# A two-block kernel on one core: the cross-attention memory loaded in feature quarters, with its transposes and splits moved between key chunks and modulation sums

## The chip, the cores and the metric

The kernel runs on one core of one Trainium2 chip. The metric is the device time of one execution in microseconds (us). The profile is one execution, recorded by the hardware profiler; its times count from the start of its span.

## The reference

Two transformer blocks run one after the other on 256 tokens with 2048 features, all in float32. What matters here is the start of the work. The program's first products belong to the cross attention of the second block (its keys depend only on the memory `mem_2`, so they can be made first) and to the modulation of the first block:

```python
# second block: cross attention over 256 memory rows
rms_norm_2(mem, norm_mem)            # (256, 2048)
k, v = split_cols_2(mem_n @ w_kv_cross, (512, 512))
# first block: modulation of context and latent
m = jax.nn.silu(cond) @ w[:, :n * D_MODEL] + b[:n * D_MODEL]
uc = ctx_s * (1.0 + sc_c) + sh_c     # then uc @ w_in_e ...
```

## The kernel before

Every large product is made to float32 precision out of three passes. A weight chunk is 512 input features by 512 output columns, 1 MB. SyncE's queue (SP) loads it into one of four slots of `weights_raw`; ScalarE (ACT, `hi`, L861) rounds it to `weights_hi`; VectorE (DVE, `lo`, L1706) subtracts to get `weights_lo`; TensorE (PE, `chunk`, L2928) then does 24 matmuls on it: 4 feature tiles by 2 token halves by 3 passes. The activations are split the same way, into `acts_hi` (L949) and `acts_lo` (L1778), after PE has transposed them (`transposes`, L3001). Four side banks take the transposes; one job is two feature tiles by two token halves, so 4 transposes.

The start of the program, which the change touches, works on three things:

- **The memory**, `memory_first` (MEM0), 256 rows by 2048 features, 2 MB. It needs 8 transpose jobs. Jobs 0 and 1 are the features of key chunk 0, jobs 2 and 3 those of key chunk 1, and so on.
- **The key chunks** 0 to 3 of `w_kv_cross` (stage `mem_k`), 1 MB each.
- **The modulation chunks** m0, m1, ... of `w_ada` (256 input features by two blocks of 512 columns each, 1 MB, loaded as two DMAs of 512 KB). They go into four slots of `modulation_weights`; PE sums them with `cond_sums` (L3024, 8 matmuls in the trace for one chunk: 4 instructions of two float32 passes), and only when chunk m is summed (`cond_used`) may SP load m+4 into its slot. m7 completes the first quarter of the modulation, m15 the second. After m7 ACT and DVE copy the rows, PE turns them into columns (`cond_cols`, L3013), and the context and latent pieces (`context_piece`, `latent_piece`, 512 KB each, loaded by GpSimd's queue, POOL) are modulated with them.

SP issues in the order written by hand in `block.sync`: it waits inside the list, so a load behind a waiting load waits too. `MEM_LOADS` and `KV_LOADS` say behind which modulation chunk a key chunk or a chunk of `w_in_e` is issued. In POOL's list the first context piece waits for `cond_used` 2 and the first latent piece for `cond_used` 6. PE's order is set by `stream(st["mem_k"], after={...})`: after key chunk 0 come jobs 4 to 7 and m0, m1; after chunk 1 come m2, m3; after chunk 2 come m4 to m7 and the columns; then chunk 3. Then the context and latent products (L3078) alternate with m8, m9 and so on, two at a time, down to m15.

A second copy of the memory, `memory_natural` (MEMN), is loaded much later, inside stage `mix`, ahead of chunk 6 of `w_mix_out` on the same queue.

Of the kernel before, what the change touches and what calls it, by code (L numbers as in the profile page):

```python
# [15 lines left out]
P = 128  # L16
T = 256
D = 2048
NB = 512
# [123 lines left out]
def build(nc, a, out, stop=None):  # L143
# [256 lines left out]
    st = {}  # L400
# [41 lines left out]
    J, n = {}, 0  # L442
# [83 lines left out]
        return CONDR[:, m % 4]  # L526

    COND_BANK = (2, 7, 5, 7)
    MEM_LOADS = {1: 2, 3: 3}
    KV_LOADS = {7: 0, 8: 1} | {8 * q + k: 4 * q + n - 4 for q in range(1, 4) for n, k in enumerate((1, 3, 5, 7), 1) if (q, n) != (1, 1)}  # L530
    KV_FIRST = 1 + max(KV_LOADS.values())
    GATE_AT = list(range(6, 19)) + [20, 23, 26]
    landed = [S(f"chunk_landed{i}") for i in range(4)]
    cond_landed = [S(f"cond_landed{i}") for i in range(8)]
    COND_IN = 16 * 2 * KT // 4
    FIRST_RANK_IN = COND_IN + 16 * (2 * KT // 8 + 1)
    PLAIN_BANK = (0, 2)
# [62 lines left out]
    @block.sync  # L600
    def _(eng):
        def load(s, blk, kc, g, slot=None):
            if not isinstance(g, int) or g >= 4:
                eng.wait_ge(lo_ready, g - 3)
            sl = slot if slot is not None else g % 4 if isinstance(g, int) else kc
            src = s.view((kc + s.rot) % s.kc, blk)
            if s.name == "lora":
                eng.dma_start(RAW[:, sl, :, 0:288], src[0]).then_inc(cond_landed[sl], 16)
                eng.dma_start(RAW[:, sl, :, 288:368], src[1]).then_inc(landed[sl], 16)
                return  # L610
            eng.dma_start(RAW[:, sl, :, 0:s.n], src).then_inc(landed[sl], 16)

        def memory(dst):
            for h in range(2):
                eng.dma_start(dst[:, :, h, :], a["mem"][0][h * P:(h + 1) * P, :].rearrange("p (b n) -> p b n", n=NB))\
                   .then_inc(S("mem_in"), 16)

        def by_chunk():

            eng.wait_ge(S("a_ab_ready"), 1)  # L620
            sa = a["scratch_a"].rearrange("(u c) t s -> c t u s", c=4)
            for c in range(4):
                r = slice(C * c, C * (c + 1))
                eng.dma_start(sa[c], AAB[r, :, r]).then_inc(S("a_ab_stored"), 16)
            eng.wait_ge(S("a_ab_stored"), 64)
            bank_full(eng, J["aqT"] + 3)
            eng.dma_start(AC[:, :, :], a["scratch_a"]).then_inc(S("a_by_chunk_in"), 16)
            eng.wait_ge(S("inverse_ready"), 1)
            eng.dma_start(a["scratch_t"], TC[:, :, :]).then_inc(S("inverse_stored"), 16)
            eng.wait_ge(S("inverse_ready"), 2)  # L630
            eng.dma_start(a["scratch_a"], TCR[:, :, :]).then_inc(S("rows_stored"), 16)
            eng.wait_ge(S("inverse_stored"), 16)
            eng.wait_ge(S("inverse_zeroed"), 2)
            sb = a["scratch_t"].rearrange("(u c) s t -> c s u t", c=4)
            for c in range(4):
                eng.dma_start(TT[C * c:C * (c + 1), :, C * (c % 2):C * (c % 2) + C], sb[c]).then_inc(S("inverse_in"), 16)
            eng.wait_ge(S("rows_stored"), 16)
            sr = a["scratch_a"].rearrange("(u c) t s -> c t u s", c=4)
            for c in (0, 2):
                eng.dma_start(TA[C * c:C * (c + 1), :, :], sr[c]).then_inc(S("rows_in"), 16)  # L640

        for s in stages:
            if s.name == "delta_y":
                by_chunk()
            if s.view is None:
                continue
            if s.own_ring:
                memory(MEM0)
                for c in range(2):
                    load(st["mem_k"], 0, c, c)  # L650
                for m in range(s.kc * s.nblk):
                    if m >= 4:
                        eng.wait_ge(S("cond_used"), m - 3)
                    for e in range(2):
                        eng.dma_start(cond_chunk(m)[:, 2 * e:2 * e + 2, :], s.view(2 * (m % 8) + e, m // 8))\
                           .then_inc(cond_landed[m % 8], 16)
                    if m in MEM_LOADS:
                        load(st["mem_k"], 0, MEM_LOADS[m], MEM_LOADS[m])
                    if m in KV_LOADS:
                        c = KV_LOADS[m]  # L660
                        load(st["ctx_kv"], KV_BLOCKS[c % 4], c // 4, st["ctx_kv"].g0 + c)
            elif s.name == "mem_k":
                pass
            elif s.name == "ctx_kv":
                for c in range(KV_FIRST, s.nblk * s.kc):
                    load(s, KV_BLOCKS[c % 4], c // 4, s.g0 + c)
            elif s.plain:
                for m in range(s.kc * s.nblk):
                    if m < 4:
                        eng.wait_ge(lo_ready, s.g0 - 3 + m)  # L670
                    elif m < 8:
                        eng.wait_ge(chunk_used, s.g0 + 2)
                    else:
                        eng.wait_ge(S("plain_used"), m - 7)
                    eng.dma_start(RAW8[:, m % 8], s.view(m % s.kc, m // s.kc)).then_inc(cond_landed[m % 8], 16)
                eng.wait_ge(S("plain_used"), s.kc * s.nblk - 4)
            elif s.loop and not s.rot:
                with eng.Fori(0, s.nblk) as i:
                    for kc in range(4):
                        load(s, i, kc, s.g0 + 4 * i + kc)  # L680
            else:
                for c, (blk, kc) in enumerate(s.order):
                    if s.name == "mix" and c == 0:
                        bank_full(eng, J["R1"] + 1)
                    if s.name == "mix" and c == 2:
                        eng.wait_ge(S("delta_y_full"), 1)
                    if s.name == "mix" and c == 6:
                        eng.wait_ge(S("y_delta"), 2)
                        memory(MEMN)
                    load(s, blk, kc, s.g0 + c, c % 4)  # L690
        if not stop:
            for h in range(2):
                rows = out[0, h * P:(h + 1) * P, :].rearrange("p (b n) -> p b n", n=NB)
                for name, b in (("out_first", 0), ("out_last", 2)):
                    eng.wait_ge(S(name), h + 1)
                    eng.dma_start(rows[:, b:b + 2, :], OUTN[:, b:b + 2, h, :]).then_inc(S("stored"), 16)
            eng.wait_ge(S("stored"), 64)
# [152 lines left out]
    def _(eng):  # L850
# [225 lines left out]
        hi(s, s.g0, 0, 0)  # L1076
        first_memory_hi(2, 3)
        hi(s, s.g0, 0, 1)
        first_memory_hi(4, 5, 6, 7)
        hi(s, s.g0, 0, 2)  # L1080
        rms_squares(MEM0, 2, MSQ)
        hi(s, s.g0, 0, 3)
        cond_rows(0)
# [616 lines left out]
    def _(eng):  # L1700
# [192 lines left out]
        lo(s, s.g0, 0, 0)  # L1893
        first_memory_lo(2, 3)
        lo(s, s.g0, 0, 1)
        first_memory_lo(4, 5, 6, 7)
        lo(s, s.g0, 0, 2)
        inverse_rms(2)
        lo(s, s.g0, 0, 3)
        cond_rows(0)  # L1900
# [1001 lines left out]
    def _(eng):  # L2902
# [114 lines left out]
        def cond_sums(*chunks):  # L3017
            for m in chunks:
                q, kp = m // 8, m % 8
                if kp == 0 and q >= 2:  # L3020
                    eng.wait_ge(S("acts_moved"), 2 * (q - 2) + 1)
                eng.wait_ge(cond_landed[m % 8], 32 * (q + 1))
                for j in range(4):
                    ins = eng.matmul(BANKS[32 * j:32 * j + 2, COND_BANK[q], :], CF[:, 2 * kp + j // 2, :],  # L3024
                                     cond_chunk(m)[:, j, :], start=(kp == 0), stop=(kp == 7))
                ins.then_inc(S("cond_used"), 1)
# [1 line left out]
        def natural(buf):  # L3028
            return lambda f, h: buf[:, f // 4, h, (f % 4) * P:(f % 4 + 1) * P]

        def first_memory(*jobs):
            transposes("memK", natural(MEM0), jobs=jobs)

        eng.wait_ge(S("consts_in"), 16)
        eng.wait_ge(S("mem_in"), 32)
        first_memory(0, 1, 2, 3)

        def first_columns():
            cond_sums(4, 5, 6, 7)
            eng.wait_ge(S("ada0_bias_in"), 32)  # L3040
            cond_cols(0)

        stream(st["mem_k"], after={0: lambda: (first_memory(4, 5, 6, 7), cond_sums(0, 1)), 1: lambda: cond_sums(2, 3),
                                   2: first_columns})

        def first_keys():
# [127 lines left out]
        def plain_rows(m):  # L3174
# [2 lines left out]
            b, kt = m // KT, m % KT  # L3177
            if kt == 0:
                eng.wait_ge(block_out, 2 * (s.b0 + b) + 2)
            eng.wait_ge(cond_landed[m % 8], COND_IN + 16 * (m // 8 + 1))  # L3180
            for j in range(4):
                ins = eng.matmul(BANKS[32 * j:32 * j + 2, PLAIN_BANK[b], :], CF[:, kt, :], RAW8[:, m % 8, j, :],
                                 start=(kt == 0), stop=(kt == KT - 1))
# [515 lines left out]

        def memory_tiles(*jobs):  # L3700
            def step():
                eng.wait_ge(S("mem_in"), 64)
                transposes("memT", natural(MEMN), jobs=jobs)
            return step

# [114 lines left out]
```

## Time and profile before

| | us |
|---|---|
| median of 3 runs (2428.3 to 2431.14) | 2428.43 |
| the profiled execution, its own time | 2428.9 |
| its span | 2427.1 |
| PE busy in the span | 2356.6 (97%) |
| DVE busy | 1442.8 (59%) |
| ACT busy | 1088.8 (45%) |
| HBM traffic over the span | 204 GB/s |

The time of an execution is 1.8 us more than its span. PE's busy time is the sum of its matmuls; with 97% it leaves some 70 us of idle time, spread over the program.

### The profile page before, as it was taken

Reading aid. Unit: us, or ns where it says so; the run is one execution under the profiler, and the core shown is the slowest. Engines: PE = TensorE matmul, PEld = TensorE weight load, DVE = VectorE, ACT = ScalarE, POOL = GpSimd, SP = SyncE. Lnnn points to the kernel's source line nnn. Section 1 sums busy time; section 2 is a strip of 40 time slices with the busy share of each in tenths; the row PEclk is TensorE's granted clock in tenths of the full one; section 3 lists DMA queues with packets and bytes.
Section 4 is the critical chain, followed back from the end, with each engine's and each line's share of the span. In section 5 each row is a group of like instructions: output and inputs, shape, how many; then the busy total and the mean of one; then the engine's idle time right before and its main releaser. Section 6 shows DMA issues by size and latency. Waiting matters only on the chain.

```text
span 2427.1 us, 29838 instructions
## 1 busy us (share of the span) xinstructions
PE 2356.6 (97%) x12212; PEld 1913.2 (79%) x12212; DVE 1442.8 (59%) x1416; ACT 1088.8 (45%) x1147; POOL 70.5 (3%) x116
## 2 busy tenths in 40 slices
PE   7999999999999999999999998999999999999998
PEld 5667887887687788887878777788788888888886
DVE  3455567656946887566667785565555545445454
ACT  4323554534643544536555352355544334334333
POOL 1000001000000000000000000000000000000000
PEclk9999999999999999999999999999999999999999
DMA  9994678857965696555545302654566565566563
GB/s 366 333 326 144 190 236 278 267 167 268 384 205 185 232 371 207 208 192 151 185 155 173 107 10 76 229 170 158 171 180 189 186 194 187 191 191 190 191 208 121
DMA packets 234019, 496.03 MB, mean 204 GB/s; under 512 B 21568, under 2 KB 23680, under 8 KB 226848
## 3 DMA queue, kind: packets, MB, share of 16 engines
q1 hardware_dynamic: 221904, 440.04, 55.2%
q0 software_dynamic: 11984, 54.13, 6.0%
q8 instruction: 97, 1.59, 0.3%
q14 instruction: 34, 0.28, 0.0%
HBM read 487.84 MB, written 6.29 MB: 204 GB/s over the span
## 4 chain that ended last, share of the span: by engine, by line
PE 87%; DVE 7%; ACT 3%; DMA 2%; issue 1%; SPq 0%; DVEq 0%; ACTq 0%
PE banks L2928 71%; PE banks L3078 5%; PE banks L3001 2%; ACT weights_hi L861 1%; PE banks L3024 1%; DVE weights_lo L1706 1%; DMA modulation_weights<-in_w_ada 1%; DMA weights_raw<-in_w_mix_out 1%; PE banks L3253 1%; PE banks L3122 1%; PE banks L3450 1%; DVE decayed_a L2021 0%; PE banks L3058 0%; PE banks L3355 0%; DVE inverse_products L2632 0%
## 5 line engine op out<-in xcount | busy, mean ns | idle before, releaser
L1706 DVE TENSOR_TENSOR weights_lo<-weights_raw,weights_hi 128x2048 fp32r<-128x2048 f32 x348 | 795.0, 2285 | 743.4 <-ACT weights_hi L861 741.7
L861 ACT ACTIVATE weights_hi<-weights_raw 128x2048 fp32r<-128x2048 f32 x348 | 664.9, 1911 | 974.1 <-PE banks L2928 892.8
L2928 PE MATMUL banks<-weights_hi,acts_hi 128*128 128x512 f32 (+1 forms) x2032 | 801.7, 395 | 12.2 <-DVE weights_lo L1706 10.7
L2928 PE MATMUL banks<-weights_hi,acts_lo 128*128 128x512 f32 (+1 forms) x2032 | 792.2, 390 | 0.0
L2928 PE MATMUL banks<-weights_lo,acts_hi 128*128 128x512 f32 (+1 forms) x2032 | 792.1, 390 | 0.0
L2928 PEld LDWEIGHTS banks<-weights_hi,acts_hi 128*128 128x128 f32 x2032 | 383.1, 189 | 102.2 <-issue 23.8
L2928 PEld LDWEIGHTS banks<-weights_hi,acts_lo 128*128 128x128 f32 x2032 | 383.2, 189 | 79.7
L2928 PEld LDWEIGHTS banks<-weights_lo,acts_hi 128*128 128x128 f32 x2032 | 383.4, 189 | 76.6 <-issue 0.5
L2928 PE MATMUL banks<-weights_hi,hidden_hi 128*128 128x512 f32 x288 | 112.3, 390 | 0.0
L2928 PE MATMUL banks<-weights_hi,hidden_lo 128*128 128x512 f32 x288 | 112.1, 389 | 0.0
L2928 PE MATMUL banks<-weights_lo,hidden_hi 128*128 128x512 f32 x288 | 112.1, 389 | 0.0
L2928 PE MATMUL banks<-weights_hi,hidden_hi_odd 128*128 128x512 f32 x248 | 96.6, 389 | 0.0
L2928 PE MATMUL banks<-weights_hi,hidden_lo_odd 128*128 128x512 f32 x248 | 96.5, 389 | 0.0
L2928 PE MATMUL banks<-weights_lo,hidden_hi_odd 128*128 128x512 f32 x248 | 96.5, 389 | 0.0
L2928 PEld LDWEIGHTS banks<-weights_hi,hidden_lo 128*128 128x128 f32 x288 | 54.1, 188 | 11.2
L2928 PEld LDWEIGHTS banks<-weights_hi,hidden_hi 128*128 128x128 f32 x288 | 54.1, 188 | 11.2
L2928 PEld LDWEIGHTS banks<-weights_lo,hidden_hi 128*128 128x128 f32 x288 | 54.1, 188 | 11.1
L2928 PEld LDWEIGHTS banks<-weights_hi,hidden_lo_odd 128*128 128x128 f32 x248 | 46.5, 188 | 9.7
L2928 PEld LDWEIGHTS banks<-weights_lo,hidden_hi_odd 128*128 128x128 f32 x248 | 46.6, 188 | 9.6
L2928 PEld LDWEIGHTS banks<-weights_hi,hidden_hi_odd 128*128 128x128 f32 x248 | 46.5, 188 | 9.6
L3078 PE MATMUL banks<-weights_hi,context_hi 128*128 128x512 f32 x128 | 50.9, 397 | 0.0
L3078 PE MATMUL banks<-weights_lo,context_hi 128*128 128x512 f32 x128 | 49.9, 390 | 0.0
(613 smaller groups left out, 2365.5 us busy)
## 6 DMA issues: line engine op xcount, KB each, us to landing
weights_raw<-in_w_in_e SPq DMA_DIRECT2D x72, 1024.0 KB, 5.7
weights_raw<-in_w_up SPq DMA_DIRECT2D x64, 1024.0 KB, 5.5
weights_raw<-in_w_down SPq DMA_DIRECT2D x64, 1024.0 KB, 5.1
weights_raw<-in_w_in SPq DMA_DIRECT2D x44, 1024.0 KB, 5.1
modulation_weights<-in_w_ada SPq DMA_DIRECT2D x64, 512.0 KB, 10.2
raw_eight<-in_w_ada SPq DMA_DIRECT2D x32, 1024.0 KB, 7.4
weights_raw<-in_w_in_o SPq DMA_DIRECT2D x32, 1024.0 KB, 6.0
gate_piece<-in_w_ada POOLq DMA_DIRECT2D x32, 512.0 KB, 5.8
```

Of the source, the lines that this page charges most:

```text
L861: eng.activation(WHI[:, c % 2, :, 0:n], RAW[:, sl, :, 0:n], ACT.Copy).then_inc(hi_ready, 1)
L1706: eng.tensor_tensor(WLO[:, c % 2, :, 0:n], RAW[:, c % 4, :, 0:n], WHI[:, c % 2, :, 0:n].bitcast(F32), ALU.subtract).then_inc(lo_ready, 1)
L2928: ins = eng.matmul(BANKS[:, par * 2 + h, 0:s.n], x[:, t, h * P:(h + 1) * P], w[:, c % 2, k, 0:s.n], start=(kc == 0 and k == 0 and m == 0), ...
L3001: ins = eng.transpose(bank(jj)[:, (f % 2) * T + h * P:(f % 2) * T + (h + 1) * P], src(f, h), ident)
L3024: ins = eng.matmul(BANKS[32 * j:32 * j + 2, COND_BANK[q], :], CF[:, 2 * kp + j // 2, :], cond_chunk(m)[:, j, :], start=(kp == 0), stop=(kp ...
L3078: ins = eng.matmul(BANKS[:, pair * 2 + h, :], x, w[:, c % 2, k, :], start=(k == 0 and m == 0), stop=(k == 3 and m == 2))
L3122: ins = eng.matmul(bank(jj)[:, k2 * DK:(k2 + 1) * DK], KD_C[:, c0 // NB, h, c0 % NB:c0 % NB + P], NAT[:, 2 + v0 // NB, h, v0 % NB:v0 % NB ...
L3253: ins = eng.matmul(dst, DECAYED[16 + d][:, 2 * hd + k2, B * P:(B + 1) * P], S0[:, d, hd, k2, :], start=False, stop=(d == 1 and k2 == 1))
L3450: ins = eng.matmul(bank(jj)[:, q * P:(q + 1) * P], A[r, f, half * P:(half + 1) * P], B[r, f, half * P:(half + 1) * P], start=True, stop=True)
```

## The change

The memory comes as four loads of 512 KB, each a quarter of the features for both token halves, with key chunks 0 and 1 and modulation chunks between them. Each quarter has a semaphore of its own, borrowed from the modulation chunks (`cond_landed` 4 to 6). On PE the transposes run a quarter at a time, and the sums of m1 and m3 move: m1 from behind key chunk 0 to behind chunk 1, m3 from behind chunk 1 to behind chunk 2. On ACT and DVE the split of key chunk 2 goes ahead of that of memory jobs 6 and 7. The later load into `memory_natural` becomes four DMAs too.

```diff
-    MEM_LOADS = {1: 2, 3: 3}
+    MEM_LOADS = {0: 2, 3: 3}
...
+    memory_landed = [S("mem_in")] + cond_landed[4:7]
+    MEMORY_IN = [0] * 4 + [16] * 3 + [0]
...
-        def memory(dst):
-            for h in range(2):
-                eng.dma_start(dst[:, :, h, :], a["mem"][0][h * P:(h + 1) * P, :].rearrange("p (b n) -> p b n", n=NB))\
-                   .then_inc(S("mem_in"), 16)
+        def memory(dst, blocks):
+            rows = a["mem"][0].rearrange("(h p) n -> p h n", p=P)
+            for b in blocks:
+                eng.dma_start(dst[:, b, :, :], rows[:, :, b * NB:(b + 1) * NB])\
+                   .then_inc(S("mem_in") if dst is MEMN else memory_landed[b], 16)
...
-                memory(MEM0)
                 for c in range(2):
+                    memory(MEM0, (c,))
                     load(st["mem_k"], 0, c, c)
...
+                    if m < 2:
+                        memory(MEM0, (m + 2,))
                     if m in MEM_LOADS:
...
-                        memory(MEMN)
+                        memory(MEMN, range(4))
...
-        first_memory_hi(4, 5, 6, 7)
+        first_memory_hi(4, 5)
         hi(s, s.g0, 0, 2)
+        first_memory_hi(6, 7)
...
-        first_memory_lo(4, 5, 6, 7)
+        first_memory_lo(4, 5)
         lo(s, s.g0, 0, 2)
+        first_memory_lo(6, 7)
...
-        eng.wait_ge(S("mem_in"), 32)
-        first_memory(0, 1, 2, 3)
+        first_memory(0)
+        first_memory(1)
...
-            cond_sums(4, 5, 6, 7)
+            cond_sums(3, 4, 5, 6, 7)
...
-        stream(st["mem_k"], after={0: lambda: (first_memory(4, 5, 6, 7), cond_sums(0, 1)), 1: lambda: cond_sums(2, 3),
+        stream(st["mem_k"], after={0: lambda: (first_memory(2), cond_sums(0)), 1: lambda: (first_memory(3), cond_sums(1, 2)),
                                    2: first_columns})
```

**SP's queue at the program's start.** Before, the rows are:

```order
L615 DMA memory_first<-in_mem 128x4x512 x2
L611 DMA weights_raw<-in_w_kv_cross 128x4x512 x2
L655 DMA modulation_weights<-in_w_ada 128x2x512 x4
L655 DMA modulation_weights<-in_w_ada 128x2x512 x4
L611 DMA weights_raw<-in_w_kv_cross 128x4x512
L655 DMA modulation_weights<-in_w_ada 128x2x512 [waits cond_used]
```

and of the change:

```order
L618 DMA memory_first<-in_mem 128x2x512
L613 DMA weights_raw<-in_w_kv_cross 128x4x512
L618 DMA memory_first<-in_mem 128x2x512
L613 DMA weights_raw<-in_w_kv_cross 128x4x512
L658 DMA modulation_weights<-in_w_ada 128x2x512 x2
L618 DMA memory_first<-in_mem 128x2x512
L613 DMA weights_raw<-in_w_kv_cross 128x4x512
L658 DMA modulation_weights<-in_w_ada 128x2x512 x2
L618 DMA memory_first<-in_mem 128x2x512
L658 DMA modulation_weights<-in_w_ada 128x2x512 x4
L613 DMA weights_raw<-in_w_kv_cross 128x4x512
L658 DMA modulation_weights<-in_w_ada 128x2x512 [waits cond_used]
```

The whole order is now quarter 0, key 0, quarter 1, key 1, m0, quarter 2, key 2, m1, quarter 3, m2, m3, key 3; it was memory, memory, key 0, key 1, m0, m1, key 2, m2, m3, key 3. Both come to 10 MB ahead of m4, and from m4 on the queue's order is the same.

**PE from its first transpose to the modulation columns.** The 24 matmuls of each key chunk stand where "..." is. Before:

```order
L3001 MATMUL banks<-constants,memory_first 128x128 [waits mem_in,consts_in,cond_ready]
L3001 MATMUL banks<-constants,memory_first 128x128 x15
...
L3001 MATMUL banks<-constants,memory_first 128x128 [waits side_free3]
...
L3024 MATMUL banks<-modulation_weights,cond 2x512 [waits cond_landed0]
...
L3024 MATMUL banks<-modulation_weights,cond 2x512 [waits cond_landed1]
...
L3024 MATMUL banks<-modulation_weights,cond 2x512 [waits cond_landed2]
...
L3024 MATMUL banks<-modulation_weights,cond 2x512 [waits cond_landed3]
...
L3024 MATMUL banks<-modulation_weights,cond 2x512 [waits cond_landed4]
```

and of the change:

```order
L3008 MATMUL banks<-constants,memory_first 128x128 [waits mem_in,consts_in,cond_ready]
L3008 MATMUL banks<-constants,memory_first 128x128 x7
L3008 MATMUL banks<-constants,memory_first 128x128 [waits cond_landed4]
...
L3008 MATMUL banks<-constants,memory_first 128x128 [waits side_free0,cond_landed5]
...
L3031 MATMUL banks<-modulation_weights,cond 2x512 [waits cond_landed0]
...
L3008 MATMUL banks<-constants,memory_first 128x128 [waits side_free2,cond_landed6]
...
L3031 MATMUL banks<-modulation_weights,cond 2x512 [waits cond_landed1]
...
L3031 MATMUL banks<-modulation_weights,cond 2x512 [waits cond_landed2]
...
L3031 MATMUL banks<-modulation_weights,cond 2x512 [waits cond_landed3]
```

Between key chunks 0 and 1 now stand 8 transposes and one modulation chunk instead of 16 and two; between chunks 1 and 2 stand 8 transposes and m1, m2 instead of m2, m3; m3 stands behind chunk 2. From m4 on PE's order is the same.

## Rows read from the trace of the kernel before

**Rows 1.** The page: the span, and each engine's busy time.
```profile
span 2427.1 us, 29838 instructions
PE 2356.6 (97%) x12212; PEld 1913.2 (79%) x12212; DVE 1442.8 (59%) x1416; ACT 1088.8 (45%) x1147; POOL 70.5 (3%) x116
```
**Rows 2.** Waits of PE, 0 to 300 us: total, times, longest.
```profile
PE banks L3001 <- DMA memory_first<-in_mem: 10.3, 1, 10.3
PE banks L2928 <- DVE weights_lo L1706: 3.4, 1, 3.4
PE banks L3013 <- DVE modulation_rows L1828: 1.6, 1, 1.6
PE banks L3024 <- DMA modulation_weights<-in_w_ada: 1.3, 1, 1.3
```
**Rows 3.** The chain of waits, 0 to 90 us: start, us, what.
```profile
17.42 8.02 PE banks L2928 x24
25.44 1.75 PE banks L3001 x16
27.19 1.83 PE banks L3024 x16
29.02 5.67 PE banks L2928 x24
...
37.16 7.77 DMA modulation_weights<-in_w_ada
...
47.62 1.92 PE banks L3013 x16
49.54 7.20 PE banks L2928 x24
...
73.40 14.36 DMA modulation_weights<-in_w_ada
```
**Rows 4.** Windows (start:end, length; last: PE clock, DMA share, GB/s).
```profile
20.00:30.00 10.00, 10.00 (x56) 6.95 (x56) 4.25 (x9) 4.08 (x9) 0.56 (x1) 1.00 1.05 387
...
38.00:40.00 2.00, 2.00 (x11) 1.65 (x10) 1.42 (x1) 0.55 (x1) 0.00 (x0) 1.00 0.96 356
...
50.00:52.00 2.00, 2.00 (x7) 1.52 (x6) 1.85 (x5) 0.67 (x1) 0.00 (x0) 0.50 1.03 340
...
64.00:66.00 2.00, 2.00 (x17) 0.98 (x6) 1.23 (x1) 2.00 (x5) 0.00 (x0) 1.00 0.91 301
66.00:68.00 2.00, 2.00 (x11) 1.62 (x10) 0.00 (x0) 1.99 (x3) 1.41 (x3) 1.00 0.95 297
68.00:70.00 2.00, 2.00 (x11) 1.65 (x10) 1.47 (x1) 0.50 (x1) 1.71 (x2) 1.00 0.98 343
...
86.00:88.00 2.00, 0.75 (x12) 0.11 (x8) 0.00 (x0) 0.71 (x2) 0.00 (x0) 1.00 1.05 385
...
106.00:108.00 2.00, 2.00 (x14) 0.92 (x16) 2.00 (x4) 0.00 (x0) 0.00 (x0) 1.00 0.07 26
```
**Rows 5.** Timeline, the load of the constants and the first latent piece.
```profile
1.95 0.55 POOL L706 DMA_DIRECT2D constants<-in_common_consts  x1
...
44.34 0.53 POOL L717 DMA_DIRECT2D latent_piece<-in_xT  x1 [14.43 <-PE banks L3024]
```
**Rows 6.** Tile constants, 0 to 30 us: from issue to landing.
```profile
DMA to landing us min/median/max: 5.6/5.6/5.6
```
**Rows 7.** Tile modulation_weights, 0 to 110 us: from issue to landing.
```profile
DMA to landing us min/median/max: 4.0/11.3/14.4
```
**Rows 8.** Timeline of PE: matmuls of chunk 3 at its start and later.
```profile
52.38 0.63 PE L2928 MATMUL banks<-weights_lo,acts_hi 128*128 128x512 f32 x1
...
55.67 0.39 PE L2928 MATMUL banks<-weights_hi,acts_lo 128*128 128x512 f32 x1
```
**Rows 9.** The chain of waits, 1530 to 1562 us, around memory_natural.
```profile
1540.32 0.59 SPq L615
...
1541.63 10.85 DMA weights_raw<-in_w_mix_out
```

More of the change, by code:

```diff
@@ L3021, in cond_sums @@
                     eng.wait_ge(S("acts_moved"), 2 * (q - 2) + 1)
-                eng.wait_ge(cond_landed[m % 8], 32 * (q + 1))
+                eng.wait_ge(cond_landed[m % 8], MEMORY_IN[m % 8] + 32 * (q + 1))
                 for j in range(4):
@@ L3029, in natural, with first_memory @@
             return lambda f, h: buf[:, f // 4, h, (f % 4) * P:(f % 4 + 1) * P]
-        def first_memory(*jobs):
-            transposes("memK", natural(MEM0), jobs=jobs)
+        def first_memory(b):
+            eng.wait_ge(memory_landed[b], 16)
+            transposes("memK", natural(MEM0), jobs=(2 * b, 2 * b + 1))
         eng.wait_ge(S("consts_in"), 16)
-        eng.wait_ge(S("mem_in"), 32)
-        first_memory(0, 1, 2, 3)
+        first_memory(0)
+        first_memory(1)
         def first_columns():
-            cond_sums(4, 5, 6, 7)
+            cond_sums(3, 4, 5, 6, 7)
             eng.wait_ge(S("ada0_bias_in"), 32)
             cond_cols(0)
-        stream(st["mem_k"], after={0: lambda: (first_memory(4, 5, 6, 7), cond_sums(0, 1)), 1: lambda: cond_sums(2, 3),
+        stream(st["mem_k"], after={0: lambda: (first_memory(2), cond_sums(0)), 1: lambda: (first_memory(3), cond_sums(1, 2)),
                                    2: first_columns})
@@ L3179, in plain_rows @@
                 eng.wait_ge(block_out, 2 * (s.b0 + b) + 2)
-            eng.wait_ge(cond_landed[m % 8], COND_IN + 16 * (m // 8 + 1))
+            eng.wait_ge(cond_landed[m % 8], MEMORY_IN[m % 8] + COND_IN + 16 * (m // 8 + 1))
             for j in range(4):
@@ L3701, in step @@
             def step():
-                eng.wait_ge(S("mem_in"), 64)
+                eng.wait_ge(S("mem_in"), 80)
                 transposes("memT", natural(MEMN), jobs=jobs)
```

## The prediction

> **What bounds the kernel now.** I read the page first: PE is busy for 2356.6 of 2427.1 us [rows 1], so the kernel is a chain of matmuls, and a change that adds and removes none of them can only move PE's idle time. PE's waits in the first 300 us say where that lies at the start: 10.3 us for the memory, 3.4 us for the split of key chunk 0, 1.6 us for the modulation rows and 1.3 us for a modulation chunk [rows 2]. The first two, 13.7 us, are what the change reaches for.
>
> The chain of waits says who pays in the end. In the first 90 us it runs twice through a DMA of the modulation: one of 7.77 us, which ends at 44.93 (the second half of m7), and one of 14.36 us, which ends at 87.76 (m15) [rows 3]. The windows say what stands behind these: the DMA engines have a share of 1.05 at 387 GB/s from 20 to 30 us, the same share at 86 to 88 us, and fall to 0.07 only at 106 us; in between I found small gaps, at 38 and at 64 to 70 us [rows 4]. So up to m15 **the DMA engines are full**. The bytes ahead of m7 and of m15 are the same in both kernels: 10 MB ahead of m4, and the same order after it. A lead that PE gains at the start is spent in waiting for m7 and m15, unless it fills gaps.
>
> **The start.** Quarter 0 is 512 KB in place of 2 MB and is first in the queue. Then the constants, which hold the identity for the transposes, come last: issued at 1.95, 5.6 us to landing, so 7.55 [rows 5, 6]. PE begins at 7.55 in place of 10.3 [rows 2]. From the first transpose to the first matmul of key chunk 0 it takes 7.1 us now (10.3 to 17.42 [rows 3]): 4 transposes, the splits of jobs 0 and 1, the splits of the key chunk. None of that changes, so chunk 0 starts at 14.65: a lead of 2.8 us. Bounds: none if the constants are later than now, 2.8 us if not.
>
> **PE from there to m3.** Chunk 0 takes 8.02; 8 transposes 0.9 (half of 1.75); one modulation chunk 0.9 (half of 1.83); chunk 1 5.67; 8 transposes 0.9; two chunks 1.8; key chunk 2 5.67; m3 0.9 [rows 3]. That ends at 14.65 + 24.8 = 39.4. Before, m3 was summed ahead of key chunk 2: the same list with 1.75 and 1.83, 5.67, and 1.83 for m2 and m3, from 17.42, ends at 36.5. So the use of m3, which frees the slot of m7, comes **2.9 us later**, although PE started 2.8 us sooner: chunk 2 and its neighbours now stand ahead of it. The splits do not hold this up. Key chunk 2 is split ahead of memory jobs 6 and 7, and ACT is idle for several us before it.
>
> **m7.** Two conditions bound its landing. By bytes: it landed at 44.93 behind full engines, and 1 MB takes 1.05 MB / 387 GB/s = 2.7 us [rows 4], so m6 can be in by 42.2 and m7 not before 44.9. By its issue: 39.4, and then at least what the fastest 512 KB load took, 4.0 us [rows 7], of which 1.35 us is its own bytes, so 2.65 us of fixed time, then 2.7 us for both halves: 44.75. These meet within 0.2 us, so the loss of slack in the issue alone costs about nothing. But the first latent piece now comes in between. It waits for the sum of m5, behind the wait for m7 before: issued at 44.34 [rows 5]. Now m4 and m5 are summed at 39.4 + 1.8 = 41.2, its 512 KB start about 43.2, and share the engines with m7's tail. Bounds: nothing, or all of its 1.35 us. I take 0.6, half of the tail's length, as two queues share. So m7 lands at 45.5, **0.6 us later than now**, in place of 2.8 us sooner.
>
> What a page says of the fixed time is another figure. The Trainium skill, "DMA: Bandwidth & Descriptors", section "Anatomy of one DMA", gives about 2.0 us for a DMA plus its bytes at 436 GB/s (it measured GpSimd's path). By that m7 issued at 39.4 would be in at about 43.8, and only the byte bound of 44.9 would be left: the term would be 0 in place of 0.6. The 4.0 us of this trace for 512 KB is above that rule's 3.2 us, and the sum goes by the trace.
>
> **TensorE's clock.** PE now hardly waits for m7 (the one wait for a modulation chunk in rows 2 is m15's), then 1.6 us for the rows [rows 2], and the granted clock then reads 0.50 at 50 to 52 us, its 1.2 GHz level [rows 4]. The matmuls there take 0.63 us against 0.39 at full clock [rows 8], and chunk 3 takes 7.20 us where others take 5.67 [rows 3]: 1.5 us lost already. In the changed kernel m3 to m6 are summed back to back from 38.5 to about 42.2, and PE then idles for 3.3 us until 45.5. If the clock falls sooner and rises at the same distance from the restart, m7's sum (0.9) and the column matmuls (1.92 [rows 3]) run slower: at half clock up to 2.8 us more. The other end is that the clock's fall misses chunk 3 this time: 1.5 us less. I take 0.5 more, the lower part of the positive side, since small matmuls are not pure array time.
>
> **From m8 to m15.** The chain is PE alone from 49.5 to 71.6, so a shift of PE there is passed on one to one, to the sums of m8 to m11 and so to the issue of m12 to m15. The engines have gaps at 64 to 70 us (shares 0.91, 0.95 and 0.98 against 1.05: 0.3 + 0.2 + 0.1 = 0.6 us), and one at 38 (0.2 us) [rows 4]. These 0.8 us are all that an earlier PE could win at m15; a later PE widens them. Past m15 nothing that the change touches is near, and the PE chain runs on with the same shift.
>
> **The second memory load.** It stands on the chain: issued at 1540.32, each DMA 0.6 us to issue, and chunk 6 of `w_mix_out` behind it lands 10.85 us after its own issue [rows 9]. Four DMAs in place of two put the issue of chunk 6 off by 1.2 us. But 512 KB take 0.6 us to issue and 1.35 us to move, so the engines never run dry and the chunk is still third by bytes: 0, with the 1.2 us as the upper bound if this cover were gone.
>
> **The sum.** 0.6 + 0.5 + 0 = 1.1 us more, on the profiled execution 2428.9 + 1.1 = 2430.0. The median of the runs is 0.5 us lower, so 2428.4 + 1.1 = 2429.5. A measurement of this kernel tells about 0.2%, 4.9 us, from no change.
>
> **Rivals.**
> - **The lead is kept.** PE starts 2.8 us sooner and stays so: 2425.7. It needs m7 and m15 to land sooner too. Against it are the full engines [rows 4]; for it only the 0.8 us of gaps. Chance 8%.
> - **The waits for m7 and m15 go as well,** because the engines move the small loads faster or the order fits better: 2.8, the 1.3, the 1.6 and 1.5 us of slow clock, 7.2 in all: 2421.2. That is faster by 0.3%. Nothing in the windows speaks for it. Chance 3%.
> - **The start does not lead.** If the constants land no sooner than 10.3, since four kinds of loads now share the first microseconds, chunk 0 starts as before, m3 is summed at 42.2, and m7 lands at 42.2 + 2.65 + 2.7 = 47.5, 2.6 us later than now: 2428.4 + 2.6 + 0.5 = 2431.5. Then the change does not do what it is shaped for. Chance 9%.
> - **Slower by the clock.** The place is m7: PE idles 3.3 us where it idled little, and the array stays at its lower level through m7's sum, the columns and all of chunk 3 (24 matmuls a 0.43 us, 10.2 in place of 7.2): 0.6 + 2.8 + 3.0 = 6.4, 2434.8. It decides from some 4.3 us of slow clock on. The Trainium skill, "TensorE: Matmul & The Clock Gate", section "HAM oscillation", warns of just this: a wait for DMA between bursts puts the array back to half clock, and the next burst starts cold. Rows 4 and 8 agree that it happens behind m7; how long it lasts here they show only for today's wait. Chance 6%.
>
> **How the numbers follow.** The forecast has 74%. Its own range is -0.8 (gaps filled, byte bound) to +1.35 + 2.8 + 1.2 = +5.4, with the upper end needing three bounds at once. With the lead kept below and a late start above, and 1 us for the spread of runs, 8 in 10 lie from 2426.2 to 2433.0. Within 0.2% (2423.6 to 2433.3): forecast, kept lead and late start, 91%. Faster 3%, slower 6%.
>
> **What would show it.** In the changed profile: PE's first wait about 7.6 us; key chunk 0 at about 14.6; chunk 2 ahead of m3; a wait of some 3 us for a modulation chunk, ending about 45.5; a DMA share dipping near 41; m15 summed at 88.5 to 89. The granted clock should read 0.50 somewhere from 45 to 54. The prediction is wrong if the sum of m15 starts before 87, or if the times part only after 90 us, or near 1550.

## The result and the profile after

The changed kernel is slower: 2435.09 us in place of 2430.15 (medians of 20 runs each), ratio 1.0021 with a 95% interval of 1.0015 to 1.0028. The prediction was 2429.5, range 2426.2 to 2433.0. So its sign was the forecast's, its size was not: 5 us in place of 1.1, outside the range. The profiled execution took 2437.3, with a span of 2435.5, 8.4 us more than that of before, while the medians differ by 5. Both numbers have to be explained. One run of the kernel e3 below took 13556 us, five times as long as any other, and is left out of every figure.

PE's waits in the first 300 us, after (total, times, longest) [rows 2]:

```profile
PE banks L3008 <- DMA constants<-in_common_consts: 8.7, 1, 8.7
PE banks L3031 <- DMA modulation_weights<-in_w_ada: 5.4, 4, 1.7
PE banks L2935 <- DVE weights_lo L1712: 3.2, 1, 3.2
PE banks L3020 <- DVE modulation_rows L1834: 1.6, 1, 1.6
```

The wait for the memory is gone, one for the constants stands in its place, and PE now waits four times for modulation chunks where it waited once. What was won at the start and more is given back there.

The chain of waits of after, 0 to 100 us (start, us, what) [rows 3]:

```profile
15.75 8.18 PE banks L2935 x24
...
39.83 1.01 PE banks L3031 x8
...
41.27 6.96 DMA modulation_weights<-in_w_ada
48.23 0.04 issue
48.28 1.93 PE banks L3031 x8
...
51.77 3.55 PE banks L3020 x16
55.32 7.15 PE banks L2935 x24
62.47 5.44 PE banks L3086 x24
...
79.07 15.02 DMA modulation_weights<-in_w_ada
```

Key chunk 0 starts 1.7 us sooner (15.75 against 17.42). m3 is summed by 40.85, not 36.5. m7 lands at 48.23, not 44.93: 3.3 us later. Its sum takes 1.93 us (before 1.08) and the columns 3.55 (before 1.92), so key chunk 3 starts at 55.32 in place of 49.54.

Windows of after (last: PE clock, DMA share, GB/s) [rows 4]:

```profile
32.00:34.00 2.00, 2.00 (x19) 0.40 (x17) 1.20 (x4) 2.00 (x5) 0.38 (x1) 1.00 0.85 314
34.00:36.00 2.00, 2.00 (x12) 1.61 (x9) 0.46 (x2) 1.97 (x3) 0.18 (x1) 1.00 0.81 178
...
46.00:48.00 2.00, 0.60 (x4) 0.00 (x0) 0.00 (x0) 0.00 (x0) 0.00 (x0) 0.50 0.96 287
...
54.00:56.00 2.00, 2.00 (x9) 1.90 (x9) 0.61 (x4) 0.20 (x1) 0.00 (x0) 0.50 1.03 398
```

and one of before:

```profile
34.00:36.00 2.00, 2.00 (x20) 0.54 (x18) 0.17 (x1) 1.88 (x3) 0.00 (x0) 1.00 1.04 398
```

At 34 to 36 us the DMA engines move 178 GB/s, less than half of the 398 of before, at a share of 0.81 against 1.04. The granted clock is 0.50, its 1.2 GHz level, from 46 to 58 us, where before only 50 to 52 read so. Around the start of this stretch PE waits three times for a modulation chunk, for m5, m6 and m7 (the brackets give the wait before each sum):

```profile
42.22 1.04 PE L3031 MATMUL banks<-modulation_weights,cond 128*2 128x512 f32 x8 [0.56 <-DMA modulation_weights<-in_w_ada]
44.79 1.81 PE L3031 MATMUL banks<-modulation_weights,cond 128*2 128x512 f32 x8 [1.53 <-DMA modulation_weights<-in_w_ada]
48.28 1.88 PE L3031 MATMUL banks<-modulation_weights,cond 128*2 128x512 f32 x8 [1.68 <-DMA modulation_weights<-in_w_ada]
```

Taking the same PE instruction in both traces gives the whole account. The changed kernel is behind by 5.8 us when the columns are done (key chunk 3 at 55.32 against 49.54), by 6.3 us at the sum of m15 (94.13 against 87.81), and so still at 300 us. Then it loses about 2 us from 670 us on, arrives 8.8 us late at `memory_natural`, loses 1.2 more there and gets back 1.6 behind 1725 us. The steps at 670 and 1725 are the clock. At the first, the same 8 matmuls of the decay products take 3.21 us after and 1.73 before, behind equal waits of 3.16 us, and the granted clock reads 0.77 to 0.80 in one and 1.00 in the other. At the second, the same 72 matmuls take 18.19 us before and 16.57 after, and the granted clock over the first 5 us reads 0.66 and 1.00. Neither place is touched by the change, and other kernels below show either reading. They explain part of why one execution differs by 8.4 and the median by 5.

### The profile page after: what moved, and what is told of

Its sections match the earlier page's. It is cut to its first block, busy times and chain, and to the rows that moved or that the text cites. A ratio compares the mean times of both kernels' runs of the same rounds, so it can differ in the third digit from the quotient of the medians.

```text
span 2435.5 us, 29844 instructions
## 1 busy us (share of the span) xinstructions
PE 2362.7 (97%) x12212; PEld 1917.5 (79%) x12212; DVE 1442.9 (59%) x1416; ACT 1088.8 (45%) x1147; POOL 70.4 (3%) x116
## 4 chain that ended last, share of the span: by engine, by line
PE 87%; DVE 7%; ACT 3%; DMA 2%; issue 1%; DVEq 0%; SPq 0%; POOL 0%; ACTq 0%; POOLq 0%
PE banks L2935 71%; PE banks L3086 5%; PE banks L3008 2%; PE banks L3031 1%; DVE weights_lo L1712 1%; ACT weights_hi L866 1%; DMA modulation_weights<-in_w_ada 1%; DMA weights_raw<-in_w_mix_out 1%; PE banks L3261 1%; PE banks L3130 1%; PE banks L3458 1%; DVE decayed_a L2028 0%; PE banks L3066 0%; PE banks L3363 0%; DVE inverse_products L2639 0%
```

## The experiments

Ratio is to the kernel before, timed alongside on the same chip; the last column is where the sum of m15 starts in the one profile of each kernel. Where an experiment changes the number of DMAs of the later load, the count that its transposes wait for changes with it; the diffs below leave this out.

| kernel | ratio (95%) | m15 summed at, us |
|---|---|---|
| before | | 87.8 |
| after | 1.0021 (1.0015 to 1.0028) | 94.1 |
| e1 sums back | 1.0014 (1.0005 to 1.0023) | 89.8 |
| e2 later load in two | 1.0017 (1.0008 to 1.0026) | 92.6 |
| e3 before, only sums moved | 1.0025 (1.0015 to 1.0035) | 94.7 |
| e4 before, later load in four | 1.0018 (1.0008 to 1.0028) | 88.2 |
| e5 only the start's loads | 1.0004 (0.9995 to 1.0013) | 89.7 |
| e6 only m3 late | 1.0010 (1.0001 to 1.0018) | 91.6 |
| e7 before, later load behind chunk 6 | 0.9979 (0.9969 to 0.9988) | 88.2 |
| e8 e5 with constants first | 1.0000 (0.9991 to 1.0009) | 88.5 |
| e9 only m1 late | 1.0011 (1.0002 to 1.0020) | 91.6 |
| e10 e7 with the load in four | 0.9981 (0.9972 to 0.9990) | 89.6 |
| e11 in four, by token half | 1.0003 (0.9994 to 1.0012) | 89.6 |
| e12 e8 with the later load of e7 | 0.9984 (0.9975 to 0.9993) | 88.3 |

### e1, the sums put back

```diff
-            cond_sums(3, 4, 5, 6, 7)
+            cond_sums(4, 5, 6, 7)
...
-   0: lambda: (first_memory(2), cond_sums(0)), 1: lambda: (first_memory(3), cond_sums(1, 2)),
+   0: lambda: (first_memory(2), cond_sums(0, 1)), 1: lambda: (first_memory(3), cond_sums(2, 3)),
```

> The changed kernel with only PE's modulation sums put back (m1 behind key chunk 0, m3 behind chunk 1); the quarter loads, their transposes and both memory loads stay. Theory A (late sums): the loads of m5 and m7 were issued late, because the sums that free their slots moved behind a key chunk, the DMA engines ran dry at 33 to 36 us, m7 landed at 48.2 and PE's clock fell in the waits. Then here m7 lands at 45 to 45.5 us, m15 is summed at 87.8 to 88.5 in place of 94.1, and the time is 4 to 6.5 us below the changed kernel: within 1.5 us of before. Theory B (small loads): the quarter loads and the crowded first microseconds delay everything behind them. Then m15 is still summed at 93 or later and the time stays 4 us or more above before.

m7 landed at 45.5 and m15 was summed at 89.8, 4.3 us sooner than in the changed kernel; the DMA share was 1.02 to 1.07 in each window from 32 to 48 us. So theory A (late sums open a gap in the loads) held in kind and not in size. 2.0 us remain at m15, 0.6 of them at m7 and the rest slow clock in the columns (2.39 us, before 1.92) and key chunk 3 (8.31, before 7.20). In the runs e1 is 2.8 us above before by the medians where the changed kernel is 4.9 above: some 2 us are gone, not the 4 to 6.5 expected, and the intervals of the two ratios overlap. Theory B (the small loads delay everything, m15 at 93 or later) does not hold in the profile.

### e3, only the sums moved

```diff
-   cond_sums(4, 5, 6, 7)
+   cond_sums(3, 4, 5, 6, 7)
...
-   0: lambda: (first_memory(4, 5, 6, 7), cond_sums(0, 1)), 1: lambda: cond_sums(2, 3),
+   0: lambda: (first_memory(4, 5, 6, 7), cond_sums(0)), 1: lambda: cond_sums(1, 2),
```

> The kernel before with only the sums of m1 and m3 moved one key chunk later; loads as before. Theory A (late sums): PE starts at 10.3 as before, m1 is summed after chunk 1, m3 after chunk 2 at about 42; m7 lands at 48 to 50, m15 is summed at 93 to 96, and the time is 5 to 9 us above before: slower than the changed kernel, whose early start is missing. Theory B (small loads): nothing but the order of sums differs, m15 is summed at 87.5 to 89 and the time is within 1.5 us of before.

The ratio is 1.0025, 5.5 us by the medians. m7 landed at 49.7, m15 was summed at 94.7. The windows of e3 show the gap bare, without the lead that softens it in the changed kernel:

```profile
34.00:36.00 2.00, 2.00 (x18) 0.34 (x17) 0.17 (x1) 1.88 (x3) 0.48 (x1) 1.00 0.04 9
36.00:38.00 2.00, 2.00 (x13) 1.66 (x10) 0.17 (x1) 1.66 (x3) 0.08 (x1) 1.00 0.83 183
```

For 2 us the engines move 9 GB/s: m4 is in, and SP asks for m5 at 35.25, when m1 has been summed. This is what theory A expected.

### e9 and e6, one late sum at a time

e9 sums m1, m2, m3 behind key chunk 1; e6 sums m1 behind chunk 0, m2 behind chunk 1, m3 behind chunk 2. Both have the later load in two.

The edit of e6 to the changed kernel, without that of the later load:

```diff
-   0: lambda: (first_memory(2), cond_sums(0)), 1: lambda: (first_memory(3), cond_sums(1, 2)),
+   0: lambda: (first_memory(2), cond_sums(0, 1)), 1: lambda: (first_memory(3), cond_sums(2)),
```

and of e9:

```diff
-            cond_sums(3, 4, 5, 6, 7)
+            cond_sums(4, 5, 6, 7)
...
-   0: lambda: (first_memory(2), cond_sums(0)), 1: lambda: (first_memory(3), cond_sums(1, 2)),
+   0: lambda: (first_memory(2), cond_sums(0)), 1: lambda: (first_memory(3), cond_sums(1, 2, 3)),
```

> The changed kernel with the later load in two and the sum of m1 back behind key chunk 0; m3 stays behind chunk 2, m2 behind chunk 1. It tells which late sum costs. If the late issue of m5 (m1's sum) made the engines run dry at 33 to 36 us and cost most, the share there is back at 1.05, and m15 is summed 1 to 2.5 us after 87.8. If the late issue of m7 (m3's sum) costs most, m15 is summed 4 to 6 us late, as in the changed kernel.

> The changed kernel with the later load in two and only m1's sum late: m1, m2 and m3 all behind key chunk 1, m3 again ahead of chunk 2. Theory (each late sum opens its own gap): the DMA share dips at 33 to 36 us (m5's load issued at about 33), no dip at 40 to 42, where the run with only m3 late had its dip (0.50); m7 lands at 46 to 47.5 and m15 is summed at 90 to 92. Rival (m3 alone matters): shares of 1.0 throughout and m15 summed as in the run with both sums back (89.8). Time 0 to 4 us above before, which the runs can hardly tell; the profile decides.

The windows of e6:

```profile
34.00:36.00 2.00, 2.00 (x10) 1.62 (x10) 1.01 (x3) 1.97 (x4) 0.00 (x0) 1.00 1.05 384
...
40.00:42.00 2.00, 2.00 (x24) 0.32 (x12) 0.13 (x1) 1.84 (x1) 0.00 (x0) 1.00 0.50 144
```

and of e9:

```profile
36.00:38.00 2.00, 2.00 (x10) 1.65 (x10) 0.33 (x2) 1.63 (x4) 0.00 (x0) 1.00 0.96 265
...
40.00:42.00 2.00, 1.41 (x12) 0.11 (x8) 1.96 (x1) 0.01 (x1) 0.00 (x0) 1.00 1.06 364
```

Each late sum has a dip of its own: m3 one at 40 to 42, m1 a shallower one at 36 to 38 (the share was expected lower and 2 us sooner; the low figure there is the rate, 265 GB/s). m7 landed at 45.9 in e6 and 46.2 in e9, against 45.3 in e5, where neither is late, and 46.9 and 48.2 in the two profiles in which both are. Both alone end with m15 at 91.6. So neither is the sole cause, and e6's own expectation, that one of them would carry it, fell: it lay between its two cases. The ratios stand in the same order (e5 1.0004, e6 1.0010, e9 1.0011, e2 1.0017), but the intervals of neighbours overlap, so this rests on one profile of each.

### e2 and e4, the later load

The edit of e2 to the changed kernel:

```diff
-                        memory(MEMN, range(4))
+                        for h in range(2):
+                            eng.dma_start(MEMN[:, :, h, :], a["mem"][0][h * P:(h + 1) * P, :].rearrange("p (b n) -> p b n", n=NB))\
+                               .then_inc(S("mem_in"), 16)
```

and of e4 to the kernel before:

```diff
-                        memory(MEMN)
+                        rows = a["mem"][0].rearrange("(h p) n -> p h n", p=P)
+                        for b in range(4):
+                            eng.dma_start(MEMN[:, b, :, :], rows[:, :, b * NB:(b + 1) * NB]).then_inc(S("mem_in"), 16)
```

> The changed kernel with only the later load of memory_natural put back to two DMAs of 1 MB. Theory A (that load costs something of its own, 1.3 us in the profile between its issue and the split of chunk 6 of w_mix_out): the first split behind it starts 12.2 us after its first issue, as before, in place of 13.4, and the time is 1.0 to 1.5 us below the changed kernel. Rival (cover holds, the 1.3 us is chance): 13.4 us still or any value from 12 to 13.5, no difference in time. The start is as in the changed kernel: m15 summed at 93 to 95.

> The kernel before with only the later load of memory_natural as four DMAs of 512 KB. If that load costs something of its own, the split of chunk 6 of w_mix_out starts about 13.4 us after the first issue in place of 12.2, and the time is 1.0 to 1.5 us above before; if the cover by bytes holds, 12.2 us and no difference. The start is as before: m15 summed at 87.8.

The chain of waits, later load: before is [rows 9]. After:

```profile
1551.17 11.37 DMA weights_raw<-in_w_mix_out
1562.56 1.92 ACT weights_hi L866
```

with the first of four issues at 1549.11; and e2, whose split of chunk 6 starts at 1560.55:

```profile
1548.01 0.66 SPq L695
1548.71 0.62 SPq L695
1549.38 11.14 DMA weights_raw<-in_w_mix_out
```

From the first issue to the split of chunk 6 it is 13.45 us after, 13.4 in e1 and 13.3 in e4, all in four; 12.2 before, and 12.35 to 12.5 in e2, e3, e5, e6, e8 and e9, all in two. Loading in four costs **1.0 us**, ten profiles without an exception. The runs agree in sign. e2's gain (0.0004 of 2430, 1 us) is of that size, but far inside its interval; e4's loss of 4.4 us, with an interval from 1.9 us up, is more. Its profile shows 1.1 us there, 0.4 at the start and some 2.5 us between 1460 and 1500, where nothing was changed and the granted clock reads 0.69 at 1474 to 1490 (0.89 before); 1.6 come back behind 1725. Why its runs lie higher than the 1.0 us stays open.

### e11, the four loads cut the other way

```diff
-                        memory(MEMN)
+                        for h in range(2):
+                            for g in range(2):
+                                eng.dma_start(MEMN[:, 2 * g:2 * g + 2, h, :], a["mem"][0][h * P:(h + 1) * P, 2 * g * NB:(2 * g + 2) * NB]
+                                              .rearrange("p (b n) -> p b n", n=NB)).then_inc(S("mem_in"), 16)
```

> The kernel before with the later load as four DMAs of 512 KB cut the other way: a token half by two neighbouring feature quarters, 4 KB runs in memory instead of 2 KB. From its first issue to the split of chunk 6: 13.3 to 13.5 us if the number of DMAs makes the 1.0 us, 12.2 to 12.5 if the cut by feature quarters does (short runs and a slow first 2 us, 211 GB/s in place of 288).

From the first issue, 1543.76, to the split of chunk 6, 1555.98, it is 12.2 us, as in two. The time is that of before (1.0003). So it is the cut, not the number. Each load by feature quarters takes 2 KB out of every 8 KB row. The windows of the two at the same distances, 2.0 and 4.0 us, from the first issue; e11:

```profile
1545.80:1547.80 2.00, 1.67 (x8) 1.31 (x8) 1.45 (x2) 1.77 (x1) 0.00 (x0) 1.00 0.91 293
1547.80:1549.80 2.00, 2.00 (x11) 1.63 (x10) 1.82 (x1) 0.15 (x1) 0.00 (x0) 1.00 1.00 353
```

and after:

```profile
1551.10:1553.10 2.00, 1.69 (x8) 1.28 (x8) 1.50 (x2) 1.70 (x1) 0.00 (x0) 1.00 0.97 252
1553.10:1555.10 2.00, 2.00 (x11) 1.65 (x10) 1.75 (x1) 0.22 (x1) 0.00 (x0) 1.00 0.93 260
```

The quarters take about as much of the engines' time and move fewer bytes in it. e11 is one profile, and whether it is the length of the runs or the number of rows that a load touches it does not tell. At the start of the program the quarters have other loads between them, and nothing like it stands out.

### e5 and e8, what the start's loads are worth

e5 is the changed kernel with the sums of e1 and the later load of e2. e8 is e5 with this in `block.gpsimd`:

```diff
-        eng.dma_start(COLS[:, :], a["cols"]).then_inc(S("cols_in"), 16)
         eng.dma_start(CONST[:, 0:COMMON], a["common_consts"]).then_inc(S("consts_in"), 16)
+        eng.dma_start(COLS[:, :], a["cols"]).then_inc(S("cols_in"), 16)
```

> The changed kernel with both the sums and the later load put back: only the quarter loads of the start, with their transposes and the earlier split of key chunk 2, remain. Theory A (the engines are full up to m15, small loads harmless): PE starts at 8.5 in place of 10.3, the lead is gone at m7, and with the sums back m15 is summed at 87.8 to 90 (1.0 to 2.1 us late in the run that also kept the later load in four); the time is within 1.5 us of before. Theory B (the loads cost of their own): 2 us or more above before.

> The kernel of e5 with the load of the constants issued ahead of that of the feature columns on GpSimd's queue. PE then starts its transposes about 0.7 us sooner (7.8 in place of 8.5). Theory A (full engines up to m15): m15 is summed at the same time as in e5 within 0.5 us, and so the time is within 1 us of e5: a lead at the start is worth nothing. Rival (the start sets the pace): 0.7 us of it reaches m15.

Both give the time of before within their intervals (1.0004 and 1.0000), as theory A expected. e5 starts key chunk 0 some 2 us sooner than before and yet has m7 at 45.4 and m15 at 89.7. The lead is spent in three waits for modulation chunks, 3.5 us, where before had one of 1.3. This is what the prediction said of full engines. In e8 PE did not start sooner: its first transpose stands 0.7 us later than in e5 (PE also waits there for `cond_ready`, which ACT makes from the feature columns, and they now come last), and m15 was summed 1.2 us sooner, for another reason:

```profile
48.02 3.55 PE banks L3022 x16
```

is the columns' line in the chain of e5, and in e8 it is

```profile
48.03 1.98 PE banks L3022 x16
```

These are the same 16 matmuls at the same time, slowed by 1.6 us in one. So e8 does not test what it was made for; it shows that the clock weighs more than 0.7 us of lead.

### e7, e10 and e12, the later load behind chunk 6

```diff
-                    if s.name == "mix" and c == 6:
+                    if s.name == "mix" and c == 7:
                         eng.wait_ge(S("y_delta"), 2)
                         memory(MEMN)
```

e10 is this with the four loads of e4, e12 is e8 with this.

> The kernel before with the later load of memory_natural issued behind chunk 6 of w_mix_out in place of ahead of it. The chain runs through that load at 1540 to 1552 us. If the 2 MB ahead of chunk 6 are what the chain pays, chunk 6 lands some 5 us sooner, PE's wait of 2.9 us there and the slow clock behind it (1.5 us) go, and the time is 3 to 4.5 us below before. Rival: chunk 7, now behind the memory, is late instead, or another wait takes the place: within 1 us of before.

> The kernel before with the later load as four DMAs and issued behind chunk 6 of w_mix_out. In four ahead of that chunk it cost 1.0 us in three profiles against six. Theory (the price is paid only because chunk 6 waits behind it): here it costs nothing, and the time is that of the run with two DMAs behind chunk 6, 5 us below before, within 1 us. Rival (the four loads cost more than this, as the runs of e4, 4.4 us above before, would have it): 2 us or more above the run with two.

> A version that may beat both kernels: quarter loads at the start, constants ahead of the feature columns, sums where they were before, and the later load in two behind chunk 6. If the start is set by the full DMA engines, the quarter loads add nothing and it is as fast as the kernel before with only the later load moved (5 us below before), within 1.5 us. If the early start is worth something once the sums are back, it is 1.5 us or more faster than that one.

e7 is **5.0 us faster than before** (2425.5 against 2430.5, ratio 0.9979, interval 0.9969 to 0.9988), the best of all. Its chain of waits there:

```profile
1541.59 2.31 DVE weights_lo L1706
1543.89 0.14 issue
1544.03 16.15 PE banks L2928 x70
```

The DMA of 10.85 us of [rows 9] has left the chain, and PE goes through three chunks without a pause. PE's waits from 1530 to 1580 us for the split fell from 3.2 us to 0.3, and three chunks take 16.6 us, where before the one behind the wait took 7.37 by itself. Against the same PE instruction of before, e7's profile goes from 1.1 us late to 3.6 early there: 4.7 us. Expected were 3 to 4.5 us. e10 gives 0.9981: in four behind chunk 6 the load costs nothing that can be told, so its price in the changed kernel is that of standing ahead of a chunk that is waited for. e12 gives 0.9984: quarter loads and an earlier start add nothing to e7.

## Why the prediction was wrong

**The start: mostly right.** Expected 2.8 us of lead, it was 1.7. The constants took 6.6 us to land in place of 5.6 [rows 6], so PE began at 8.7, not at 7.55. The 5.6 was one reading and the shortest: in the profiles in which the constants are issued at 1.95 it is 6.2 to 6.8 with the changed start, and 6.1 to 6.6 in the other five with the start of before. The rest of the 7.1 us path held.

**m3's use: right but for that.** Expected 39.4, it was 40.85: 1.1 of it from the constants.

**m7: this is the step that failed.** The prediction bounded m7 by bytes ("m6 can be in by 42.2") and by its own issue, found the two within 0.2 us, and concluded that "the loss of slack in the issue alone costs about nothing". The byte bound assumed engines full up to m6. They were not. The sum of m1 had moved as well, to 33.2 us, so SP asked for m5 about the time the queue ran out of m4. The prediction gave the issue of m7 its arithmetic and that of m5 none; the diff moved both. In e3 the gap is 2 us long, in e6 and e9 each late sum shows its own. m7 landed 3.3 us late in place of 0.6.

What the step left out can be measured by its own arithmetic, the end of m3's sum and then 2.65 + 2.7 us. The last lines of the chain to m7 (start, us, what) in e6, where only m3 is late, and in e2, whose start is that of the changed kernel:

```profile
40.95 4.96 DMA modulation_weights<-in_w_ada
```

and

```profile
40.60 6.25 DMA modulation_weights<-in_w_ada
```

In e6 m3 is summed by 40.52, which gives 45.9, and m7 landed at 45.91. Where m1's sum is late as well, m7 came later than the arithmetic says: 48.23 against 46.2 in the changed kernel, 46.85 against 45.5 in e2, 49.68 against 48.1 in e3. I put these 2.0, 1.3 and 1.6 us down to what e6 does not have, the late sum of m1 and with it the late issue of m5. The rest of the 3.3, 1.3 us, is the late sum of m3, for which the prediction took nothing because it expected that sum 1.45 us sooner. The gap also varies: two executions of one start had m7 3.3 and 1.9 us late. The latent piece, which I charged with the 0.6, was issued at 43.6, 2.4 us after m7's second half; no run tells its share apart.

**The clock: right in kind, too small.** I took 0.5 us of a bound of 2.8. m7's sum lost 0.85 and the columns 1.6, so 2.5 in the profile. The prediction had m3 to m6 summed back to back and one idle stretch of 3.3 us. PE waited three times, 0.6, 1.5 and 1.7 us, with one chunk's sum in between. The clock was at its lower level before m7 came (0.50 at 46 to 48 us), and stayed there for the columns. Of the page that I weighed there ("TensorE: Matmul & The Clock Gate" of the Trainium skill, "HAM oscillation": waits for DMA between bursts put the array back to half clock) the trace shows this outcome: the sum of m6, behind waits of 0.6 and 1.5 us, already takes 1.81 us in place of 1.04. It was set down as a rival with 6%; the rival's own price of all of chunk 3 at half clock did not come (7.15 us, 7.20 before). But the columns vary with the start of before too: 1.92 us in its profile, in e4 and in e7, 3.15 and 3.22 in e10 and e11, whose starts are the same, with m15 summed 1.7 us later. The starts like that of before average 0.9 us above its profile (0, 0.4, 0.4, 1.7, 1.8), those with both sums late and the lead 5.5 us (6.3, 4.8). The difference, 4.6, is my estimate of the change at m15, from five profiles and two, and with the 1.0 us of the later load it gives 5.6, against 5 in the runs.

**The second load: the cover argument was right, and the price was elsewhere.** SP issued four DMAs in 2.0 us, and the engines were not short of work. They moved fewer bytes on rows cut into quarters: 1.0 us, which the prediction put at 0 with a bound of 1.2 for another reason. e11 issues four DMAs just as late and pays nothing. Times that part near 1550 were among the prediction's own signs of being wrong.

**The stretch past m15: right, up to the later load.** From m15 to 670 us the lag stays at 6.3 us, and the lead at the start was worth nothing (e5, e12).

## What to carry over

Where a queue is kept full by slots that a consumer frees, ask of every moved consumer when the next load is asked for, not only of the one on the chain: one late release opens a gap, and the loads behind it land later. Before bringing an engine's start forward, look for the transfer that it will meet next: against full DMA engines an earlier start turns into waiting, and waiting may cost clock as well. A prefetch that is not needed for a while (here issued at 1540 and first used at 1575 us) and stands in the queue ahead of a load that the chain waits for is worth moving behind it: here 5 us, as much as the change lost.

## What the runs showed of the hardware

- 2 MB in four loads by feature quarters (2 KB of each 8 KB row) put the chunk behind them off by 1.0 us against two loads of whole rows (three profiles against seven); four loads by token half (4 KB runs), by nothing (one profile).
- Executions of one kernel spread over some 9 us (2425.6 to 2434.6 before). Part of what two profiles differ by is TensorE's clock at short stalls: the same 8 matmuls near 670 to 680 us took 1.73 us at a granted clock of 1.00 and 3.21 at 0.77 to 0.80, and the same 16 column matmuls 1.92 to 3.22 in the five profiles with the start of before, 3.54 or 3.55 in six with other loads or sums there.
- The first matmuls of key chunk 0 take 0.63 us, as those do where the granted clock reads 0.50 [rows 4, 8], while the granted clock of their own window (18 to 22 us before) reads 1.00. There the duration tells more than the reading of the clock.
